# DeltaNet chunk inverse: one of its two copies is transposed from the other instead of being multiplied out

## The reference

```python
kk = jnp.einsum('cbhik,cbhjk->cbhij', kc, kc)
A = jnp.where(strict, bc[..., :, None] * kk * gamma, 0.0)
Tm = lax.linalg.triangular_solve(eye + A, eye, left_side=True, lower=True, unit_diagonal=True)
u = jnp.einsum('cbhij,cbhjv->cbhiv', Tm, vc * bc[..., None])
w = jnp.einsum('cbhij,cbhjk->cbhik', Tm, kc * (bc * jnp.exp(decay))[..., None])
...
v_new = u_c - w_c @ S
o = q_dec @ S + attn @ v_new
S = S * dl + k_tail.T @ v_new          # chunk after chunk
```

## Time and profile before

| | |
|---|---|
| median of three runs | 3499.21 us (3496.5 to 3500.31) |
| the profiled execution | 3489.25 us |
| its span, first to last instruction | 3487.2 us |
| mean granted TensorE clock | 0.968 of 2.4 GHz |
| instructions | 56485 |

### The profile page before, as it was taken

One profiled execution on the slowest core, in us unless ns is written; L12 is line 12 of the kernel. 1 busy time (PEld: TensorE's weight loads), 2 busy tenths in 40 slices (PEclk: granted clock), 3 DMA queues, 4 the chain that ended last, 5 costly groups with the idle time before them and its releaser, 6 DMA issues. The chain is left out here.

```text
span 3487.2 us, 56485 instructions
## 1 busy us (share of the span) xinstructions
PE 3208.5 (92%) x20770; PEld 3101.6 (89%) x20770; DVE 1367.2 (39%) x2586; ACT 848.1 (24%) x1773; POOL 1225.7 (35%) x1048
## 2 busy tenths in 40 slices
PE   5999999999986889999999979999877999999998
PEld 4889888888976889999999969999776999999997
DVE  4465556555543242233223243434323323223323
ACT  2343443343342111101110124444412110110012
POOL 3333333333313454433443152132044533434330
PEclk8999999999998999999999989999888999999999
DMA  3000100100002111111111120111021211111111
GB/s 126 25 12 22 28 21 7 28 21 21 8 3 83 42 49 52 44 48 36 54 48 42 49 44 20 23 34 32 2 98 30 61 48 42 48 48 44 40 36 50
DMA packets 200992, 137.26 MB, mean 39 GB/s; under 512 B 32056, under 2 KB 192624, under 8 KB 200368
## 3 DMA queue, kind: packets, MB, share of 16 engines
q1 hardware_dynamic: 200880, 135.63, 13.3%
HBM read 120.98 MB, written 14.63 MB: 39 GB/s over the span
## 5 line engine op out<-in xcount | busy, mean ns | idle before, releaser
L89 PE MATMUL ps<-act_hi,ffn_hi 128*128 128x352 f32 x2112 | 681.9, 323 | 3.7 <-DVE act_lo L235 3.7
L90 PE MATMUL ps<-act_lo,ffn_hi 128*128 128x352 f32 x2112 | 676.9, 321 | 0.0
L91 PE MATMUL ps<-act_hi,ffn_lo 128*128 128x352 f32 x2112 | 676.3, 320 | 0.0
L143 POOL TENSOR_TENSOR ffn_hi<-ffn_stage,one 128x512 fp32r<-128x512 f32 x264 | 291.4, 1104 | 813.5 <-PE ps L91 765.8
L89 PEld LDWEIGHTS ps<-act_hi,ffn_hi 128*128 128x128 f32 x2112 | 396.2, 188 | 4.4 <-ACT ffn_silu L403 4.2
L90 PEld LDWEIGHTS ps<-act_lo,ffn_hi 128*128 128x128 f32 x2112 | 396.8, 188 | 0.2
L91 PEld LDWEIGHTS ps<-act_hi,ffn_lo 128*128 128x128 f32 x2112 | 395.8, 187 | 0.0
L862 POOL TENSOR_TENSOR gdn_mt_level<-gdn_mt,joins 128x384 f32<-128x384 f32 x168 | 178.3, 1066 | 592.2 <-DVE gdn_qd L1301 305.0
L420 DVE TENSOR_TENSOR ffn_hid<-ffn_silu,ps 128x352 f32<-128x352 f32 x132 | 68.8, 522 | 783.7 <-PE ps L91 783.7
L145 POOL TENSOR_TENSOR ffn_lo<-ffn_stage,ffn_hi 128x512 fp32r<-128x512 f32 x264 | 342.2, 1296 | 20.6
L430 DVE TENSOR_TENSOR x<-x,ps 128x352 f32<-128x352 f32 x528 | 269.4, 519 | 187.1 <-PE ps L91 187.1
(11 more groups left out here) (310 smaller groups left out, 5861.0 us busy)
## 6 DMA issues: line engine op xcount, KB each, us to landing
ffn_stage<-in_ffn_w_gu SPq DMA_DIRECT2D x88, 512.0 KB, 3.9
ffn_stage<-in_ffn_w_down SPq DMA_DIRECT2D x44, 512.0 KB, 3.5
gdn_stage<-in_gdn_w_in SPq DMA_DIRECT2D x32, 512.0 KB, 4.3
x_kept<-x SPq DMA_DIRECT2D x2, 4224.0 KB, 12.7
x<-x_kept SPq DMA_DIRECT2D x2, 4224.0 KB, 13.2
ml_stage<-in_ml_w_in SPq DMA_DIRECT2D x16, 512.0 KB, 4.6
load_rows<-in_x_prompt SPq DMA_DIRECT2D x8, 512.0 KB, 4.5
gdn_out_stage<-in_gdn_w_out SPq DMA_DIRECT2D x8, 512.0 KB, 4.5
```

The source lines that it names most:

```text
L89: pe.matmul(out, w_hi, rhs_hi, start=first, stop=False)
L90: pe.matmul(out, w_hi, rhs_lo, start=False, stop=False)
L91: return pe.matmul(out, w_lo, rhs_hi, start=False, stop=last)
L143: nc.gpsimd.tensor_tensor(hi, st, one, ALU.mult).then_inc(self.hi_done, 1)
```

## The change

The first copy of the inverse is no longer multiplied out and subtracted in levels 1 to 5. Instead PE transposes the second copy at the start of the next level (`turn_z`, levels 2 to 6) into bank 4, and ACT copies bank 4 into `z[.., 0]` (`copy_z`). `join_w` of those levels waits for that copy, and stands after the two pieces of place A instead of before them. DVE's subtraction L1323 goes. Level 0 stays as it is, and level 1 still reads the copy that level 0 made.

```diff
+            def turn_z(t, r, l):
+                pe.wait_ge(z_done, t * 24 + (r * 8 + l + 1))
+                for i in range(BATCHES):
+                    mm = pe.transpose(ps[:, 4, i * P:(i + 1) * P], z[:, r % 2, 1, i], tk.ident[:])
+                mm.then_inc(z_turned, 1)
+
             def join_w(t, r, l):
-                pe.wait_ge(z_first, t * 18 + (r * 6 + l)) if l else pe.wait_ge(z_done, t * 24 + (r * 8 + 1))
+                if l >= 2:
+                    pe.wait_ge(z_copied, t * 15 + (r * 5 + l - 1))
+                else:
+                    pe.wait_ge(z_first, t * 3 + (r + 1)) if l else pe.wait_ge(z_done, t * 24 + (r * 8 + 1))
...
-                if 0 < l < LEVELS - 1:
-                    for i in range(BATCHES):
-                        mm = pe.matmul(ps[:, 4, i * P:(i + 1) * P], z[:, par, 1, i], wz[:, i], start=True, stop=True)
-                    mm.then_inc(pz_done, 1)
...
                     for l in range(LEVELS):
-                        if r < BATCHES:
+                        if r < BATCHES and l >= 2:
+                            turn_z(t, r, l)
+                        if r < BATCHES and l < 2:
                             join_w(t, r, l)
                         pieces(r, l, "A")
+                        if r < BATCHES and l >= 2:
+                            join_w(t, r, l)
                         if r > 0 and 2 * l < 9:
                             chain_step(t, r - 1, 2 * l)
...
+            def copy_z(t, r, l):
+                act.wait_ge(z_turned, t * 15 + (5 * r + l - 1))
+                nc.scalar.copy(z[:, r % 2, 0], ps[:, 4, 0:3 * P].rearrange("p (i c) -> p i c", i=3)).then_inc(z_copied, 1)
...
                     for l in range(LEVELS):
+                        if r < BATCHES and l >= 2:
+                            copy_z(t, r, l)
                         if r < BATCHES:
                             copy_w(t, r, l)
...
-                elif l < LEVELS - 1:
-                    dve.wait_ge(pz_done, t * 36 + (12 * r + 2 * l))
-                    nc.vector.tensor_tensor(flat(0), flat(0), ps[:, 4, 0:3 * P], ALU.subtract).then_inc(z_first, 1)
-                dve.wait_ge(pz_done, t * 36 + (12 * r + min(2 * l + 1, 12)))
+                dve.wait_ge(pz_done, t * 21 + (7 * r + l + 1))
                 nc.vector.tensor_tensor(flat(1), flat(1), ps[:, 5, 0:3 * P], ALU.subtract).then_inc(z_done, 1)
```

More of the change, by code:

```diff
@@ L793, in gdn_phase @@
         level_masked, z_first, z_done = sem("level_masked"), sem("z_first_done"), sem("z_done")
+        z_turned, z_copied = sem("z_turned"), sem("z_copied")
         wz_done, wz_copied, pz_done = sem("wz_done"), sem("wz_copied"), sem("pz_done")
@@ L926, in prepare @@
                         pe.wait_ge(z_done, t * 24 + 8 * r)
+                        pe.wait_ge(z_copied, t * 15 + 5 * r)
                     for i in range(BATCHES):
```

## The result

The changed kernel takes 3580.56 us (median of four runs, 3575.11 to 3582.24) beside 3497.86 for the kernel before on the same chip: ratio 1.0241, interval [1.0222, 1.026], so 83 us slower. The forecast was 3598, 99 slower. The profiled execution took 3582.24 us, its span is 3580.2.

The account below looks back on a forecast made before the run. PE's own issue time was taken to bound the loop heads. With the two waits, heads 0 to 6 add 75.8 us and the last head 15.8, together +91.6, on the median 3591; half clock adds 7: 3598 us, range 3562 to 3632.

Parts of the forecast that it names:

- Rival A: Heads 0 to 6: pieces and steps cover both waits, PE's saving comes through; about 3470 us; chance 3%.
- E: Rival: the turn's transposes run as full matmuls (0.67 us), +0.35 for each of 120, 3640 us; chance 5%.
- Turns behind a norm's sum or a three-matmul step: Sign in the loop heads: no new idle time on PE before these transposes; the step or sum covers the subtraction.
- Wait 1: PE waits for ACT's `wz` copy behind the moved `join_w`: 1.41 us to its reader; with T, +0.40 a level without step.
- T: The turn's three transposes at a level's start, before the pieces of place A: 0.24 us of PE time a group.
- Wait 2: Transposes wait for DVE's subtraction on the second copy: 1.74 us against 1.15 before, +0.70 in levels without a chain step.
- Rival B: Same waits with shorter hand-overs and no more half clock: 0.25 us less in some 90 levels, near 3568; chance 15%.
- level 3 of batch 2: Loop heads: ACT is late from SiLU work, so `join_w` waits until 2.44 us instead of 1.30; +0.6.
- The last head: Nothing covers the hand-overs: T with its copy adds 1.14 us fifteen times, net 15.8; four levels at half clock add 7.
- Three signs: Bare loop levels 4.4 to 4.6 us, last head near 100 to 107, time outside the inversions unmoved.
- The loop heads' clock: Added half clock in the loop heads: put at 0, other end one 6.8 us stretch in each, 24 us.
- Rival D: Half clock spreads: last head throughout (+26), the others once each (up to +24); 3617 to 3641 us; chance 10%.

Follow-up runs that it names:

- no_waits: Changed kernel with transposes reading the first copy and `join_w` ahead of the pieces, so neither wait remains (not the inverse): 3452.12 us, ratio 0.9877 to before.
- wait_wz: Changed kernel with transposes reading the first copy, `join_w` still behind the pieces, so only the wait for `wz` remains (not the inverse): 3525.38 us, ratio 1.0087 to before.
- turn_matmul: Changed kernel with each transpose of the turn written as a full float32 multiplication by the identity, in all heads: 3607.42 us, ratio 1.0322 to before.
- last_twice: Changed kernel with the turn's three transposes issued twice over in the last head alone: 3572.38 us, ratio 1.0242 to before; second run 3568.96 us.
- split: Changed kernel with one of the two pieces of place A put behind `join_w`, levels 2 to 6: 3568.19 us, ratio 1.0212 to before.

## Why the prediction was right, and where it was off

**Right.** The bound, the sign and both mechanisms: PE bounds the loop heads, its saving comes through (`no_waits`, -42), and two hand-overs that had been covered cost more than that. Rival A falls with `wait_wz`, E with `turn_matmul`. Turns behind a norm's sum or a three-matmul step start without a wait, as said.

**Wait 1** was sized nearly right. The terms of the forecast that belong to it and to T give +29 in heads 0 to 6 (75.8 less the 46.6 of wait 2); `wait_wz` has +33.7 against before. W to Z1 was put at 1.41 and is 1.40 in the changed kernel, 1.47 in `wait_wz`.

**Wait 2 is the mis-sized term.** The prediction has 1.63 + 2.39 + 2.39 = 6.4 a head and 8.2 in head 0, which has no sums: 46.6 us in heads 0 to 6; the chip has 907.3 - 880.5 = 26.8. In a bare level it was to cost +0.70 and costs 0.31. Three things make the difference. From Z1 to T it is 1.58, not 1.74: in the row that I took it from the earlier trace rows DVE started 1.04 after a waited Z0 and the next product came 0.15 after the subtraction; here DVE starts 0.97 after Z1 (596.71 - 595.74) and T comes 0.05 after its end (597.27 to 597.32). That is 0.16. Second, I set it against 1.15, PE's own time from an unwaited Z1 to T, but wait 1 makes Z1 a waited group, and from that PE needs 1.26 (rows of `wait_wz`): 0.11 that comes with wait 1 already, which I had too small by it. Third, with T waiting, T to W takes 0.06 more and W to Z1 0.07 less, where I had +0.11. The whole bare level was put at 4.56 and is 4.33: 0.16 of that from Z1 to T and 0.06 from T to W (1.35, not 1.41). Rival B, shorter hand-overs, named both of these, and its 3568 lies nearer to the 3580.56 than the forecast's 3598 does.

One smaller slip: for level 3 of batch 2 the prediction has W wait until 2.44, but its own rows give 1.83 + 0.48 + 0.06 = 2.37; the chip has 2.34 (T at 622.54, W at 624.88).

**The last head** was right in sum, +24.8 against 22.8, and nearly in its parts. `last_twice`'s second run had it at full clock in 100.9; less its fifteen added groups of 0.33 the changed head would take 96.0, so half clock cost it 13.4, or 0.29 for each of the 46 us (0.31 by `split`). At that rate the 14 us of before cost 4.0. The chain's own lengthening is then 96.0 - 80.6 = 15.4 (forecast 15.8), and the clock's 9.4 (forecast 7). That the 7 came so near is luck: with `split`'s 26 us at half clock the same head has a clock term of some 3.5. Two levels of it, at half clock and at full:

```profile
1080.23 0.90 PE L948 MATMUL ps<-ident,gdn_z 128*128 128x128 f32 x3 [0.72 <-DVE gdn_z L1341]
1081.17 0.48 ACT L1164 COPY gdn_z<-ps 128x384 f32<-128x384 f32 x1 [2.38 <-PE ps L948]
1081.80 1.62 PE L962 MATMUL ps<-gdn_z,gdn_mt_level 128*128 128x128 f32 x6 [0.66 <-ACT gdn_z L1164]
1083.98 1.65 PE L973 MATMUL ps<-gdn_z,gdn_wz 128*128 128x128 f32 x6 [0.57 <-ACT gdn_wz L1159]
...
1110.37 0.55 PE L948 MATMUL ps<-ident,gdn_z 128*128 128x128 f32 x3 [0.72 <-DVE gdn_z L1341]
1110.95 0.48 ACT L1164 COPY gdn_z<-ps 128x384 f32<-128x384 f32 x1 [1.83 <-PE ps L948]
1111.58 0.91 PE L962 MATMUL ps<-gdn_z,gdn_mt_level 128*128 128x128 f32 x6 [0.66 <-ACT gdn_z L1164]
1113.05 0.94 PE L973 MATMUL ps<-gdn_z,gdn_wz 128*128 128x128 f32 x6 [0.57 <-ACT gdn_wz L1159]
1114.09 0.55 DVE L1341 TENSOR_TENSOR gdn_z<-gdn_z,ps 128x384 f32<-128x384 f32 x1 [3.78 <-PE ps L973]
1114.70 0.55 PE L948 MATMUL ps<-ident,gdn_z 128*128 128x128 f32 x3 [0.72 <-DVE gdn_z L1341]
```

T to Z1 takes 3.75 at half clock and 2.68 at full; ACT's copy takes 0.48 in both. From T's start to W it is 1.21, forecast 1.14. What I did not foresee is the pattern: not four levels here and there, but one stretch of 30.7 us.

Three signs that the prediction named were missed by a little: bare levels in the loop are 4.33 (4.4 to 4.6), the last head is 109.4 (100 to 107), and the profiled time outside the inversions moved, by the clock as far as the rows tell.

**The loop heads' clock** was put at 0 and cost some 5 us: of the six heads 1 to 6, three had one stretch of 3.4 us at half clock before, five have one after. Head 0 had one stretch before, of 5.9 at its very start, and has three of 3.4 after. Heads with one take 129.3 us after, the one without 127.7; at that rate the 11 us more at half clock in heads 0 to 6 cost 5. Rival D is right in kind, but far smaller than it was put.

**Open:** why the clock's fall comes as one long stretch in batch 0 of the last head and leaves batch 1's levels, alike but for the chain steps, at 1.00. Both runs of the changed kernel have it in the same place, and `split`, with the same instructions, has levels 2 to 5 of batch 0 at full clock, and half clock again only from its level 6 on, for 6.8 us. What in the heads ahead decides it is not known.

## What to carry to other kernels

Count a level of a chain twice, once as PE's issue time and once as the chain of hand-overs, and take the longer: work taken off PE pays only as long as the second stays under the first, and a filler can cover one hand-over at a time. When two waits follow each other, size the second against the level with the first already in it. And before moving work off an engine, look at the largest wait that stands in the list already; here it was one operand away from 45 us.

## What the runs showed of the hardware

A DVE operation of three operands on 128x128 float32 took 0.34 us with one of them in PSUM, 72 times out of 72 (340 to 352 ns). With both tensors in SBUF it took 0.94 in the mean. In the last head, where POOL is not splitting weights, three of them together take 1.00 to 1.11; in a loop head 3.04, beside POOL's operations. The timeline of before, batch 2 of a loop head:

```profile
576.63 3.04 DVE L1318 SCALAR_TENSOR_TENSOR gdn_z<-gdn_wz,gdn_head_gates,gdn_z 128x128 f32<-128x128 f32 x3
577.10 1.09 POOL L143 TENSOR_TENSOR gdn_hi<-gdn_stage,one 128x512 fp32r<-128x512 f32 x1
578.26 1.26 POOL L145 TENSOR_TENSOR gdn_lo<-gdn_stage,gdn_hi 128x512 fp32r<-128x512 f32 x1
```

The Trainium skill has this in "SBUF — State Buffer", section "Who interferes with whom": a VectorE instruction with two SBUF inputs contends with a GpSimd instruction that reads SBUF, one with a single SBUF input does not, outside VectorE's two-port modes. The rows agree.

On the half clock: the same last head, instruction by instruction, took 109.4 us with 46 of them at half clock (two runs) and 103.0 with 26 (`split`). In a head bound by hand-overs each us at half clock cost 0.31 by this pair; in a loop head, where PE sets the pace, it was 0.47 (1.6 us for a stretch of 3.4). One profile of such a head is not enough to put its half clock down to its own instructions.
